# One decoder step on one core: the value products of paged attention as four column tiles of 512 columns

## What is computed

```
def diff_attn_sample(q, k_new, v_new, k_past, v_past, lam):
    s = concat([diff_scores(q, k_past), diff_scores(q, k_new)])   # per head two score sets
    w = diff_probs(s, mask, lam)             # softmax of one set minus lam times softmax of the other
    return (einsum('bhqk,bkhv->bqhv', w[..., :p], v_past)
            + einsum('bhqk,bkhv->bqhv', w[..., p:], v_new))
```

## Time and profile before

| | us |
|---|---|
| median of 3 executions (lowest, highest) | 1993.85 (1989.64, 1997.44) |
| the profiled execution | 1993.27 |
| its span, first to last instruction | 1991.4 |
| TensorE busy in the span | 1675.7 |
| VectorE busy | 1267.2 |
| ScalarE busy | 831.9 |
| first and last load of the cache issued | 363.8, 1076.3 |
| last value product | 1093 |

### The profile page before, as it was taken

The page is one execution under the profiler, slowest core; times in us unless marked ns, Lnnn a source line. Parts: engine busy times, 40 slices in busy tenths (PEclk is TensorE's granted clock), DMA queues, the critical chain, the costliest instruction groups (busy, mean ns, idle before and its releaser), DMA issues. The chain is left out here.

```text
span 1991.4 us, 37111 instructions
## 1 busy us (share of the span) xinstructions
PE 1675.7 (84%) x14983; PEld 1280.3 (64%) x14983; DVE 1267.2 (64%) x1685; ACT 831.9 (42%) x1415; POOL 401.4 (20%) x362
## 2 busy tenths in 40 slices
PE   6999999478888888877777699708999999999990
PEld 4677777356777756555555255406888888888870
DVE  4321441578687588678782233347898889888954
ACT  4322222012322143343332322116778778777850
POOL 0000000212333243333332000031221222022103
PEclk9999999668999798798989799758999999999995
DMA  6062121887999899999998541008999999999957
GB/s 203 11 249 89 43 77 45 294 298 284 376 366 417 311 417 417 388 414 407 417 406 363 171 190 64 22 19 334 392 401 407 404 403 403 406 403 405 402 203 272
DMA packets 105169, 577.14 MB, mean 290 GB/s; under 512 B 14913, under 2 KB 20417, under 8 KB 52049
## 3 DMA queue, kind: packets, MB, share of 16 engines
q0 software_dynamic: 46512, 302.28, 37.9%
q1 hardware_dynamic: 58528, 272.98, 35.3%
HBM read 531.41 MB, written 43.81 MB: 289 GB/s over the span
## 5 line engine op out<-in xcount | busy, mean ns | idle before, releaser
L2020 DVE TENSOR_TENSOR e_l<-first_w,e_h 128x1024 fp32r<-128x1024 f32 x256 | 294.6, 1222 | 10.0 <-ACT e_h L2017 9.6
L1330 DVE STREAM_TRANSPOSE d_ring<-d_ring 128x2048 f32<-128x2048 f32 x128 | 292.2, 2298 | 11.8 <-DMA d_ring<-in_cache_k,d_rows 11.1
L2017 ACT CAST e_h<-first_w 128x1024 fp32r<-128x1024 f32 x256 | 250.3, 1048 | 83.8 <-POOLq L2089 42.8
L810 PE MATMUL ps<-d_ring,d_qb 128*32 128x128 f32 x4096 | 163.4, 311 | 103.8 <-DVE d_ring L1330 103.6
L790 POOL DMA_INDIRECT d_ring<-in_cache_k,d_rows x128 | 122.9, 960 | 533.2 <-DVE d_rows L1283 265.0
L810 PEld LDWEIGHTS ps<-d_ring,d_qb 128*32 128x32 f32 x4096 | 124.0, 124 | 136.8 <-DVE d_ring L1330 113.0
L1979 PE MATMUL ps<-e_h,e_xh 128*128 128x512 f32 x512 | 206.7, 404 | 3.5 <-DVE e_xl L2029 3.5
L1981 PE MATMUL ps<-e_h,e_xl 128*128 128x512 f32 x512 | 203.7, 398 | 0.0
L1980 PE MATMUL ps<-e_l,e_xh 128*128 128x512 f32 x512 | 203.6, 398 | 0.0
L321 PE MATMUL ps<-wh,xh 128*128 128x512 f32 (+1 forms) x432 | 173.7, 402 | 0.0
L322 PE MATMUL ps<-wl,xh 128*128 128x512 f32 (+1 forms) x432 | 171.1, 396 | 0.0
(11 more groups left out here) (314 smaller groups left out, 2698.3 us busy)
## 6 DMA issues: line engine op xcount, KB each, us to landing
first_w<-in_w_down SPq DMA_DIRECT2D x32, 2048.0 KB, 9.0
first_w<-in_w_up SPq DMA_DIRECT2D x62, 1024.0 KB, 8.1
first_w<-in_w_gate SPq DMA_DIRECT2D x62, 1024.0 KB, 10.9
ys_d<-e_y SPq DMA_DIRECT2D x32, 512.0 KB, 10.0
cat<-in_w_in SPq DMA_DIRECT2D x6, 2048.0 KB, 9.6
ys_d<-cat POOLq DMA_DIRECT2D x1, 8192.0 KB, 33.5
kT<-in_x_prompt SPq DMA_DIRECT2D x8, 512.0 KB, 6.8
m_wout<-in_w_out SPq DMA_DIRECT2D x2, 2048.0 KB, 10.0
```

What stands on the lines that cost most here:

```text
L810: mm = pe.matmul(k.ps[32 * h:32 * h + 32, SC, part], qb[:, b % 2, i, h, :], keys[:, :, h, i, :], start=i == 0, stop=i == BLOCKS - 1)
L1330: dve.transpose(in_ring((KEYS, b, g)), in_ring((KEYS, b, g))).then_inc(s_kt, 1)
L2017: return act.copy(h13[:, :, kk, :], w13[:, :, kk, :])
L2020: return dve.tensor_tensor(l13[:, :, kk, :], w13[:, :, kk, :], h13[:, :, kk, :].bitcast(F32), ALU.subtract)
```

## The change

The value products take another form. For row r of a load the stationary operand is now 32 columns of `pT`, the 8 probabilities of all 4 heads for one row number, and the moving one is all 512 value columns. Their output is partitions 32r to 32r+31 of `OUT`: the column tile belongs to r, no longer to the head. It holds all pairs of heads, of which one in four is wanted. So that the 32 columns lie side by side, `turn` no longer transposes against the identity but makes plain products with a permutation matrix `swap`. At the end of a sequence VectorE copies the bank to `u` (`keep_sums`), and TensorE makes one product with `alike` for the sums and four with `pick`, each of which adds up the four r for one head and picks its rows (`close_sums`); only then `output` runs. `open_sums` is gone: the product with the new tokens, 512 columns wide, opens the sum. `pT` has 4 pieces instead of 5, so the last turned piece of a sequence waits for the last values of the one before, and its copy stands a slot later. Ahead of the last sequence's values there are 3 empty slots, at the end 2 more.

```diff
-    KEPT_P = SUPERS + 1
+    KEPT_P = SUPERS
...
         if b == SAMPLES:
-            slots += early + late
+            slots += [None] * 3 + early + late
...
-    slots += [None] * 2
+    slots += [None] * 4
...
                     if x == 0:
-                        mm = pe.transpose(k.ps[0:NS, SC, 0:P], s_new[:, b, :], ident)
+                        mm = pe.matmul(k.ps[0:NS, SC, 0:32], s_new[:, b, :], swap[:, 0:32], start=True, stop=True)
                     else:
                         for r in range(GROUP):
                             a = 512 * (x - 1) + r * P
-                            mm = pe.transpose(k.ps[:, SC, r * P:(r + 1) * P], s[:, a:a + P], ident)
+                            mm = pe.matmul(k.ps[:, SC, r * P:(r + 1) * P], s[:, a:a + P], swap, start=True, stop=True)
                     mm.then_inc(s_t, 1)
-                def open_sums(b):
-                    pe.wait_ge(s_exp, (b + 1) * PIECES)
-                    pe.wait_ge(s_tk, b * PIECES + 1)
-                    if b:
-                        pe.wait_ge(s_ok, b)
-                    pe.matmul(k.ps[:, OUT, 0:DV + PIECES], alike[:], sz[:, b % 2, :], start=True, stop=False, skip_group_check=True)
-                    for h in range(HEADS):
-                        pe.matmul(k.ps[32 * h:32 * h + 8, OUT, 0:DV], pTn[:, 32 * h:32 * h + 8], k.new_v[:, h * DV:(h + 1) * DV],
-                                  start=False, stop=False, skip_group_check=True)
                 def values(b, x):
+                    out = k.ps[:, OUT, :]
                     if x == 0:
-                        open_sums(b)
+                        pe.wait_ge(s_tk, b * PIECES + 1)
+                        if b:
+                            pe.wait_ge(s_ok, b)
+                        pe.matmul(out[0:32], pTn[:], k.new_v[:], start=True, stop=False, skip_group_check=True)
...
-                        for h in range(HEADS):
-                            mm = pe.matmul(k.ps[32 * h:32 * h + 8, OUT, 0:DV],
-                                           pT[:, (b * SUPERS + x // 4) % KEPT_P, r, 32 * h + 8 * a:32 * h + 8 * a + 8],
-                                           v[:, r, h * DV:(h + 1) * DV], start=False, stop=x == GROUPS - 1 and r == GROUP - 1,
-                                           skip_group_check=True)
+                        mm = pe.matmul(out[32 * r:32 * r + 32], pT[:, (b * SUPERS + x // 4) % KEPT_P, r, a:a + 32], v[:, r, :],
+                                       start=x == 0 and r > 0, stop=x == GROUPS - 1, skip_group_check=True)
                     mm.then_inc(s_pv, 1)
+
+                def close_sums(b):
+                    pe.wait_ge(s_u, b + 1)
+                    pe.wait_ge(s_exp, (b + 1) * PIECES)
+                    pe.matmul(k.ps[:, OUT, DV:DV + PIECES], alike, sz[:, b % 2, :], start=True, stop=True)
+                    for h in range(HEADS):
+                        mm = pe.matmul(k.ps[32 * h:32 * h + 8, OUT, 0:DV], pick[:, 8 * h:8 * h + 8], u[:, h * DV:(h + 1) * DV],
+                                       start=True, stop=True)
+                    mm.then_inc(s_cl, 1)
...
+                        if n == at[VALUES, b, GROUPS - 1] + 3:
+                            close_sums(b)
...
-                        elif after == 6:
+                        elif after == 7:
                             keep_turned(b, 4)
...
+                def keep_sums(b):
+                    dve.wait_ge(s_pv, (b + 1) * GROUPS)
+                    if b:
+                        dve.wait_ge(s_cl, b)
+                    dve.tensor_copy(u[:], k.ps[:, OUT, :]).then_inc(s_u, 1)
...
                         if n == at[VALUES, b, GROUPS - 1] + 2:
+                            keep_sums(b)
+                        elif n == at[VALUES, b, GROUPS - 1] + 4:
                             output(b)
```

More of the change, by code:

```diff
@@ L102, in constant_table @@
     put("alike", (t[:, None] // 32 == t[None, :] // 32) & (t[:, None] % 8 == t[None, :] % 8))
+    put("swap", np.eye(P).reshape(P, 4, 4, 8).transpose(0, 2, 1, 3).reshape(P, P))
+    put("pick", np.arange(32)[None] == t[:, None] % 32)
     at, n = {}, 0
@@ L631, in mixers @@
     meta_at = lin_at[-1] + 11
-    att_at, left = [], len(slots) - 10 - (meta_at + 2) - 3 * len(STEP)
+    att_at, left = [], len(slots) - 12 - (meta_at + 2) - 3 * len(STEP)
     for n, (i, h) in enumerate(STEP):
@@ L642, in mixers @@
         ring = sb("d_ring", [P, RING, GROUP * W])
-        alike = sb("d_alike", [P, P])
+        fixed = sb("d_fixed", [P, 2 * P + 32])
+        alike, swap, pick = fixed[:, 0:P], fixed[:, P:2 * P], fixed[:, 2 * P:2 * P + 32]
         rows = sb("d_rows", [P, 2, SAMPLES, GROUPS], I32)
@@ L651, in mixers @@
         nm = sb("d_nm", [P, 2])
-        sz = sb("d_sz", [P, 2, DV + PIECES])
+        sz = sb("d_sz", [P, 2, PIECES])
         r2 = sb("d_r2", [P, 2])
         pT = sb("d_pT", [P, KEPT_P, GROUP, P])
-        pTn = sb("d_pTn", [NS, P])
+        pTn = sb("d_pTn", [NS, 32])
+        u = sb("d_u", [P, W])
         o = sb("d_o", [P, 2, DV])
@@ L699, in mixers @@
                                                           sem("d_t_"), sem("d_tk"), sem("d_pv"))
+        s_u, s_cl = sem("d_u_"), sem("d_cl")
         s_ok, s_ch, s_b, s_back, s_z = sem("d_ok"), sem("d_ch"), [sem("d_b0"), sem("d_b1")], sem("d_back"), sem("d_z")
@@ L745, in _ @@
                 sp.dma_start(spread, io["consts"][:, KEPT:KEPT + P]).then_inc(s_con, 16)
-                sp.dma_start(alike[:], io["consts"][:, KEPT + P:KEPT + 2 * P]).then_inc(s_con, 16)
+                sp.dma_start(fixed[:], io["consts"][:, KEPT + P:KEPT + 3 * P + 32]).then_inc(s_con, 16)
                 old_states = io["state_gla"][:, 0].rearrange("b (x e) k v -> e k b x v", e=2)
@@ L1108, in exponentials @@
                         if b >= 2:
-                            act.wait_ge(s_pv, (b - 2) * GROUPS + 1)
+                            act.wait_ge(s_cl, b - 1)
                     piece = s_new[:, b, :] if x == 0 else s[:, 512 * (x - 1):512 * x]
                     act.activation(piece, piece, ACT.Exp, scale=scale, bias=nm[:, b % 2:b % 2 + 1],
-                                   accum_out=sz[:, b % 2, DV + x:DV + x + 1]).then_inc(s_exp, 1)
+                                   accum_out=sz[:, b % 2, x:x + 1]).then_inc(s_exp, 1)
                 def keep_turned(b, x):
@@ L1118, in keep_turned @@
                             act.wait_ge(s_pv, (b - 1) * GROUPS + 1)
-                        act.copy(pTn[:], k.ps[0:NS, SC, 0:P]).then_inc(s_tk, 1)
+                        act.copy(pTn[:], k.ps[0:NS, SC, 0:32]).then_inc(s_tk, 1)
                     else:
@@ L1343, in shared_maximum @@
                     dve.tensor_scalar(nm[:, b % 2:b % 2 + 1], mtT[:, 0:1], -scale, None, ALU.mult).then_inc(s_nm, 1)
+                def keep_sums(b):
[3 more added lines that the diff above has]
+                    dve.tensor_copy(u[:], k.ps[:, OUT, :]).then_inc(s_u, 1)
                 def output(b):
-                    dve.wait_ge(s_pv, (b + 1) * GROUPS)
+                    dve.wait_ge(s_cl, b + 1)
                     chain.link(dve.reduce_sum(r2[:, 0:1], k.ps[:, OUT, DV:DV + PIECES], axis=X))
```

2 lines of the change are left out of this document (1 added, 1 removed).

## The result

The changed kernel takes **2019.71 us** (median of 4 runs, 2015.6 to 2022.31); the kernel before, run beside it, 1994.76 us. The ratio is 1.0126 with a 95% interval of 1.0098 to 1.0154: **25 us, 1.3%, slower**. The forecast was 2007, the range 1991 to 2020. The direction came out as forecast, the size is twice the 12 us expected; the time lies at the very top of the range.

The account below looks back on a forecast made before the run. Most of the changed part was taken to wait for cache loads, with TensorE costing time before 690 us; 2 + 4 + 2 + 4 + 1.7 = 13.7 us on 1993.27 gave 2007 us, range 1991 to 2020.

Parts of the forecast that it names:

- The value products: Products of the 128 loads: a quarter of the instructions but the same columns to stream, so a gain of 0.
- the rival of 2240 us: Value products: four column tiles of 512 columns do not overlap, 3.4 us a load instead of 0.86; chance 0.03.
- The turning: Plain products instead of transposes cost 0.53 us more for each of four large pieces, 2.1 us a sequence.
- The rival of a four times dearer turning: Plain turning products cost four times the transposes, 7.6 us more a sequence, 2025 us in all; chance 0.12.
- The clock: Rival: plain products lift TensorE's half clock in sequence 0's turning, dips go, kernel faster at 1982 us; chance 0.10.
- The opening and closing: Wide new-token product, five-column product and four picks replace L832 and L834: 0.6 us a sequence more on TensorE.
- The end: Behind the last products: VectorE's copy, five products at half clock and two handovers, 1.7 us, all on the path.
- sequence 0: Its turning at half clock, with nothing to cover the added time: 2 us reach the end.
- sequences 1 and 2: Turning shortly before DMA dips, partly taken from TensorE's waits for VectorE: 4 us of 2 x 3 reach the end.
- sequence 7: Chain and attention before its values free no buffer, against a queue of three loads: 4 us reach the end.
- Sequences 3 to 6: DMA share full, so added TensorE time is mostly covered: 2 of 12 us reach the end (0 to 8).
- The cover: Loads under way hide late TensorE work behind 690 us: no dips there, 7.5 us to landing taken as three loads.

Follow-up runs that it names:

- before_plain_turning: Kernel before with plain products against the identity instead of transposes in the turning; 2013.11 us, ratio 1.0090.
- new_values_lean: Changed kernel with transposes for the turning, 5 turned pieces, no empty slots ahead of the last sequence, prompt attention at its old slots; 2002.81 us, ratio 1.0043.
- lean_plain_turning: new_values_lean with the plain turning products of the change again; 2019.09 us, ratio 1.0119.
- after_old_places: Changed kernel with the steps of prompt attention at the slots they had before; 2029.11 us, ratio 1.0203.
- before_new_places: Kernel before with the steps of prompt attention where the change has them, no empty slots; 2006.92 us, ratio 1.0058.
- before_empty_slots: Kernel before with the empty slots of the change and its places for prompt attention, still 5 turned pieces; 2003.5 us, ratio 1.0044.
- before_plain_new_places: Kernel before with plain turning products and prompt attention at the change's places together; 2013.21 us, ratio 1.0088.
- turn_by_transpose: Changed kernel with the turning made by transposes again, ScalarE's copy putting the columns in order; 2014.0 us, ratio 1.0096.
- before_2us_elsewhere: Kernel before with nine products of the identity with itself ahead of every sequence's ninth scores; 2001.82 us, ratio 1.0038.
- lean_no_closing: new_values_lean without VectorE's copy of the bank and the five closing products; 1997.35 us, ratio 1.0022.

## Why the prediction was half right

**The value products** were priced at a gain of 0: 143.6 us for 146.4, and 143.6 again when cut in four. A load's 8 records take 1.07 us at full clock (forecast 1.04). One after another they would take 3.4 (0.43 each). That four column tiles of 512 columns run at once is thereby shown; the rival of 2240 us is out.

**The turning** was priced right: 1.16 us a piece, from L1055, measured as 1.16, and 2.1 us a sequence is 16.8, measured 17.5. The rival of a four times dearer turning is out. Timeline of the changed kernel in sequence 5:

```profile
903.41 1.16 PE L829 MATMUL ps<-d_fixed,d_s 128*128 128x128 f32 x8
904.61 0.58 ACT L1131 COPY d_pT<-ps 128x512 f32<-128x512 f32 x1 [1.06 <-PE ps L829]
905.34 1.13 PE L829 MATMUL ps<-d_fixed,d_s 128*128 128x128 f32 x8 [0.77 <-ACT d_pT L1131]
```

The Trainium skill (TensorE: Matmul & The Clock Gate, Terms, under xbus) has transposes four times faster for FP32. Measured over the whole group it is 40.1 to 22.6, 1.8 times, and here the measurement counts.

**The clock** did not rise. At half clock a piece takes 2.05 us where transposes took 1.09, and the window 450 to 460 us stands at 0.55, before at 0.61. By the rule of the Trainium skill that transposes do not count as busy work (same page, Part 4) the denser plain products should have lifted it; this trace does not agree: `before_plain_turning` has 0.59 there, and `new_values_lean`, with transposes, 0.53.

**The opening and closing** were undersized: 9.2 us on TensorE over 8 sequences, 1.15 a sequence, not 0.6. The product with the new tokens was to take 0.86 and takes 1.04 (8.3 by 8); the five-column product 0.50 and not 0.2; the picks 0.54 and not 0.3 to 0.4. **The end** was forecast at 1.7 and is 1.95.

**What reaches the end is the step that failed.** Against the table: sequence 0 had 2 and lost 2.5 (1.4 more were gone ahead of it); sequences 1 and 2 had 4 and lost 4.5; sequence 7 had 4 and lost 1.0; the end 1.7 and 1.9. Sequences 3 to 6 were given "2 of 12" and lost **17.9**. That row is the step, and three things in it were wrong.

*The moved attention was put at nothing.* The forecast counted time added to TensorE and said of the prompt's attention that it "is not added, only moved ahead", for sequence 7 alone. It is moved from sequence 3 on. How much later than in the kernel before GpSimd issues the loads, in us, in one profiled execution of each kernel (713.1, 1002.5 and 1076.3 us before for loads 112, 224 and 255):

| Kernel | by load 112 | from 112 to 224 | from 224 to 255 |
| --- | --- | --- | --- |
| before_plain_turning (old places) | 6.2 | 3.9 | 6.4 |
| new_values_lean (old places) | 8.2 | 0.6 | 3.2 |
| lean_plain_turning (old places) | 12.7 | 7.9 | 7.8 |
| after_old_places | 7.3 | 12.2 | 11.9 |
| before_new_places | 3.8 | 13.5 | -0.5 |
| before_empty_slots (new places) | -0.5 | 15.2 | 2.6 |
| before_plain_new_places | 5.3 | 17.9 | 0.2 |
| turn_by_transpose (new places) | 3.1 | 8.7 | 1.4 |
| the changed kernel (new places) | 8.4 | 17.9 | 4.6 |

The middle column is sequences 3 to 6. With no work added the new places alone lose 13.5 us there, plain turning alone 3.9 (of 8.4 added, so about half is covered), and both together 17.9, as the changed kernel does. Pairs of kernels that differ by the turning alone differ there by 4 to 9 us, pairs that differ by the places alone by 6 to 14. So the largest row comes from the places first and from turning second. A single execution of a kernel can be 5 us and more off its median (`turn_by_transpose` was profiled in the shortest of its four), so the split is no finer than that.

*The cover was read wrongly.* "No dip behind 690 us" overlooks the window 830 to 840 us, where the kernel before has a share of 0.94 and 331 GB/s. And 7.5 us to landing are not three loads under way: the load at 459.4 us, issued to DMA engines that stood still (share 0.00 in 450 to 460 us), takes 5.8 us by itself. L790, the load issued in 459 to 460, and those issued from 700 to 1076 us, before:

```profile
DMA to landing us min/median/max: 5.8/5.8/5.8
...
DMA to landing us min/median/max: 7.5/10.0/15.0
```

At 2.5 us a load the least of this stretch is less than one load of cover (1.7 us), the median less than two (4.2). After, L795 in sequence 5's turning (902 to 911 us), where the earlier trace rows had 13.5, and from 700 to 1107 us:

```profile
DMA to landing us min/median/max: 7.6/7.7/7.9
...
DMA to landing us min/median/max: 5.5/9.6/14.1
```

What takes the depth at sequence 5 is again the places. The same loads in `before_new_places` (895 to 901 us) and in `before_plain_turning` (885 to 894 us):

```profile
DMA to landing us min/median/max: 7.7/7.8/7.9
...
DMA to landing us min/median/max: 14.3/14.3/14.3
```

*VectorE's waits* of 79.5 us ahead of the scores were to take part of the added time. Of time in the turning they took nothing (`before_plain_turning`, 81.3); of time ahead of the scores they took 7 of 18.8 (`before_2us_elsewhere`).

**Sequence 7** was to lose 4 us by a pause without a free buffer, seen as dips between 1050 and 1070 us. In the changed kernel the DMA share is 1.01 from 1050 to 1090 us, and the closing (from 1086 us) and the product with the new tokens (1088.5) fall into these two windows:

```profile
1080.00:1090.00 10.00, 8.71 (x71) 4.03 (x69) 6.13 (x18) 5.18 (x19) 2.81 (x3) 1.00 1.01 417
1090.00:1100.00 10.00, 9.96 (x67) 3.89 (x62) 2.45 (x6) 2.12 (x7) 3.61 (x4) 0.83 0.99 387
```

That pause was covered but for little.

**How the parts combine** is measured for the whole kernel, not explained. Turning is worth 17.6 us in the kernel before and 15 to 16 between the two lean kernels, but 6 in the changed kernel. The places cost 12.7 in the kernel before (7.8 with the empty slots, 11.6 with these and the ring of four), and 0.2 beside plain turning: in the table what both together lose more in sequences 3 to 6 they lose less before and behind. So the lean kernels reach the loss of the whole change by another way, with plain turning (15 to 16) and the new products' form with its closing (8.6), and 25 us in the changed kernel cannot be divided among its parts. That the changed kernel is slower, and what each part costs by itself, is shown. That the time still falls into the range is luck: the upper end came from the dearer turning, which is out.

**Open:** why `after_old_places` is slower than the changed kernel; why the moved attention opens the dips, which wait it runs into; why 17 of the 23.0 us elsewhere vanish when the waits account for 7; what the 4.0 us left in `lean_no_closing` are, the product with the new tokens in its wide form being the nearest, 8.3 us for 3.4. Turning in halves, so that ScalarE's copy of one runs beside the turning of the other, was not tried.

## What to carry to other kernels

Work that is "only moved" has a price of its own: where several engines follow one common order, try the move alone before forecasting it at nothing (here 13.5 us of dips with no work added). A DMA share of 9 tenths or 1.0 does not tell how much added time is covered. Look at the time from issue to landing over the whole stretch, its least too, against what a load takes when the DMA engines stand still (5.8 us here); the difference, in transfers, is the cover, and it was under one load where the forecast saw three. Ask of each added microsecond which wait it stands ahead of: ahead of a wait for another engine it was partly paid back (6.1 of 23.0 us arrived), in a chain that the next scores wait for it was not (17.6 of 17.3). And the busy time of these products went with their columns, not with their number, so that a rearrangement which needs its operand turned by plain products instead of transposes must first earn back the turning, 40.1 us for 22.6.

## What the runs showed that was not expected

Shifting the prompt's attention by up to three slots, with no work added or taken, costs 12.7 and 13.2 us of 1994, later and earlier; by one slot later it costs 5.9 by the median, of executions that fall into two groups. The parts of a change can hide each other: +17.6 and +12.7 alone are +17.8 together. And TensorE's clock did not follow the kind of work in sequence 0's turning: 0.61 and 0.53 in 450 to 460 us with transposes (before, `new_values_lean`), 0.59, 0.55 and 0.50 with plain products (`before_plain_turning`, after, `lean_plain_turning`).
